# Value products of the first layer: hi and lo weights side by side in two passes, and a bank read per head

## What is computed

```python
p = jax.nn.softmax(logits, axis=-1).astype(v.dtype)
return jnp.einsum('bhqk,bhkd->bhqd', p, v)           # MLA; the MoBA heads likewise
...
mixed = jnp.concatenate([mla_out, moba_out], axis=-1) @ ab_w_out[e]
```

## Time and profile before

| | |
|---|---|
| time, median of 3 runs (lowest to highest) | 1370.87 us (1370.07 to 1371.33) |
| the profiled execution: its own time, its span | 1372.31 us, 1370.5 us |
| busy share: PE, PEld, DVE, ACT, POOL | 95%, 80%, 54%, 40%, 19% |
| mean granted TensorE clock | 0.981 of 2.4 GHz |
| value products of the first layer | 192 matmuls from 95.6 to 278.7 us |

### The profile page before, as it was taken

One profiled execution on the slowest core, in us unless ns is written; L12 is line 12 of the kernel. 1 busy time (PEld: TensorE's weight loads), 2 busy tenths in 40 slices (PEclk: granted clock), 3 DMA queues, 4 the chain that ended last, 5 costly groups with the idle time before them and its releaser, 6 DMA issues.

```text
span 1370.5 us, 17699 instructions
## 1 busy us (share of the span) xinstructions
PE 1308.7 (95%) x6599; PEld 1098.5 (80%) x6599; DVE 744.7 (54%) x997; ACT 553.9 (40%) x885; POOL 258.4 (19%) x206
## 2 busy tenths in 40 slices
PE   7978999999999999999998999987999999999997
PEld 5666888889888888888987888866988888888885
DVE  4776655428654454322386888783475544443223
ACT  4456566546322332222355544453453222322112
POOL 0533100016211111000141112211441111110002
PEclk9989999999999999999999999998999999999998
DMA  5412233122333333333231113110224333333331
GB/s 154 121 29 62 62 85 85 38 86 72 114 92 95 104 92 90 98 94 91 77 88 47 47 46 88 50 47 14 87 73 120 92 94 105 92 107 93 92 93 61
DMA packets 190503, 112.34 MB, mean 82 GB/s; under 512 B 13696, under 2 KB 184773, under 8 KB 190446
## 3 DMA queue, kind: packets, MB, share of 16 engines
q1 hardware_dynamic: 188636, 106.81, 27.1%
q0 software_dynamic: 640, 2.10, 0.5%
q10 hardware_dynamic: 1170, 2.66, 0.5%
HBM read 109.43 MB, written 4.74 MB: 83 GB/s over the span
## 4 chain that ended last, share of the span: by engine, by line
PE 83%; DVE 8%; ACT 4%; issue 2%; POOL 2%; DMA 0%; POOLq 0%; DVEq 0%; ACTq 0%; SPq 0%
PE banks L386 25%; PE banks L388 25%; PE banks L387 25%; PE banks L1661 3%; PE banks L1579 1%; DVE w_lo L381 1%; DVE softplus L1636 1%; PE banks L1408 1%; PE banks L1691 1%; ACT softplus L1620 1%; PE banks L435 1%; DVE u_lo L667 1%; DVE tf L657 1%; DVE logits L1370 0%; POOL rope_tmp L1117 0%
## 5 line engine op out<-in xcount | busy, mean ns | idle before, releaser
L381 DVE TENSOR_TENSOR w_lo<-w_raw,w_hi 128x1024 fp32r<-128x1024 f32 (+2 forms) x200 | 287.1, 1439 | 277.2 <-ACT w_hi L374 277.0
L386 PE MATMUL banks<-u_hi,w_hi 128*128 128x512 f32 (+1 forms) x1112 | 426.0, 383 | 7.4 <-DVE w_lo L381 4.3
L388 PE MATMUL banks<-u_hi,w_lo 128*128 128x512 f32 (+1 forms) x1112 | 419.6, 377 | 0.0
L387 PE MATMUL banks<-u_lo,w_hi 128*128 128x512 f32 (+1 forms) x1112 | 419.2, 377 | 0.0
L374 ACT ACTIVATE w_hi<-w_raw 128x1024 fp32r<-128x1024 f32 (+2 forms) x200 | 205.8, 1030 | 264.2 <-PE banks L388 264.2
L386 PEld LDWEIGHTS banks<-u_hi,w_hi 128*128 128x128 f32 x1112 | 210.5, 189 | 48.3 <-issue 6.8
L388 PEld LDWEIGHTS banks<-u_hi,w_lo 128*128 128x128 f32 x1112 | 210.3, 189 | 38.8
L387 PEld LDWEIGHTS banks<-u_lo,w_hi 128*128 128x128 f32 x1112 | 210.6, 189 | 38.1 <-issue 1.0
L860 POOL TENSOR_TENSOR up<-up,gate 128x512 f32<-128x512 f32 x44 | 71.8, 1632 | 375.5 <-DVE up L886 358.4
L841 ACT ACTIVATE gate<-gate 128x512 f32<-128x512 f32 x44 | 27.8, 632 | 202.3 <-DVE gate L882 202.3
L1678 POOL TENSOR_TENSOR stick_lo<-softplus,stick_hi 128x1280 fp32r<-128x1280 f32 x15 | 44.2, 2948 | 191.4 <-DVE stick_hi L1674 191.4
(11 more groups left out here) (244 smaller groups left out, 2010.0 us busy)
## 6 DMA issues: line engine op xcount, KB each, us to landing
w_raw<-in_ffn_w_gate_up_dram SPq DMA_DIRECT2D x88, 512.0 KB, 3.8
w_raw<-in_ffn_w_down_dram SPq DMA_DIRECT2D x30, 512.0 KB, 3.7
w_raw<-in_sb_w_qkv_dram SPq DMA_DIRECT2D x24, 512.0 KB, 3.9
w_raw<-in_ab_w_in_dram SPq DMA_DIRECT2D x17, 512.0 KB, 3.8
w_raw<-in_ffn_w_down_dram SPq DMA_DIRECT2D x16, 448.0 KB, 3.7
w_raw<-in_ab_w_out_dram SPq DMA_DIRECT2D x8, 512.0 KB, 4.1
w_raw<-in_sb_w_out_dram SPq DMA_DIRECT2D x8, 512.0 KB, 4.9
bias_by_distance<-bias_rows ACTq DMA_DIRECT2D x1, 2560.0 KB
```

The source lines that it names most:

```text
L381: dve.tensor_tensor(wl[:, c.slot, 0:w], raw[:, c.slot, 0:w], wh[:, c.slot, 0:w].bitcast(F32), ALU.subtract).then_inc(w_lo, 1)
L386: nc.tensor.matmul(o, lh, rh, start=start, stop=False, skip_group_check=True)
L387: nc.tensor.matmul(o, lh, rl, start=False, stop=False, skip_group_check=True)
L388: return nc.tensor.matmul(o, ll, rh, start=False, stop=stop, skip_group_check=True)
```

## The change

- The values get one tile `va` with, for each head, 128 columns: v_hi in the head's own 64 columns (64e on) and v_lo in the other 64. The zeros, and GpSimd's two memsets for them, are gone. A filler keeps the other tiles where they were.
- A value product is two passes instead of three, 8 matmuls instead of 12: all 128 columns by probsT_hi, then by probsT_lo. The output bank holds the head's main rows at 64e and the correction rows (v_lo's products) in the other half.
- The bank is started and read for each head by itself. ScalarE copies the main rows to `oh`, and the correction rows to `sqt` at the main rows' place. VectorE subtracts `oh` from the main rows into `acc` (`o_read_dve`, which frees the bank), and then adds `sqt` to give `ol` (`o_dve`). All of these have 64 rows.
- Order: `o_act` stands at the end of every step, not of odd ones; `o_read_dve` for head hh - 1 stands in front of probsT_lo of head hh, and its `o_dve` behind it. Each head's product after the first waits for `o_read` of the head before. `out_pe` waits for `o_dve` of head 15.

```diff
-            vh = sb(at0, "v_hi", [P, 2, TT, 192], F32R)
-            vl = sb(at0, "v_lo", [P, 2, TT, 192], F32R)
+            va = sb(at0, "v", [P, 2, 2, TT, P], F32R)
+            sb(at0, "beside_v", [P, 1024])
...
+        def v_half(buf, e, lo):
+            at = HD * (e ^ lo)
+            return va[:, buf, e, :, at:at + HD]
...
         def pv_pe(pe, hh):
             p, e = hh // 2, hh % 2
             pe.wait_ge(pt_lo, hh + 1)
             if e == 0:
                 pe.wait_ge(pj_read, order[("vt", p, 0)] + 1)
-                if p:
-                    pe.wait_ge(o_lo, p)
-            values(bank(O_BANK), (vh, vl), p % 2, e, pth, ptl, 0).then_inc(pv_done, 1)
+            if hh:
+                pe.wait_ge(o_read, hh)
+            for j in range(TT):
+                w, at = T - P * j, COL_AT[j]
+                for n, x in enumerate((pth, ptl)):
+                    mm = nc.tensor.matmul(bank(O_BANK)[:, P * j:T], va[:, p % 2, e, j, :], x[:, at:at + w],
+                                          start=(j == 0 and n == 0), stop=(j == TT - 1 and n == 1),
+                                          skip_group_check=True)
+            mm.then_inc(pv_done, 1)
+
+        def o_act(act, hh):
+            p, e = hh // 2, hh % 2
+            act.wait_ge(pv_done, hh + 1)
+            act.activation(oh[p][head_rows(e), :], bank(O_BANK)[head_rows(e), :], ACT.Copy)
+            if hh >= 2:
+                act.wait_ge(o_lo, hh - 1)
+            act.activation(sqt[head_rows(e), :], bank(O_BANK)[head_rows(1 - e), :], ACT.Copy).then_inc(o_hi, 1)
+
+        def o_read_dve(dve, hh):
+            p, e = hh // 2, hh % 2
+            dve.wait_ge(o_hi, hh + 1)
+            if hh >= 2:
+                dve.wait_ge(o_lo, hh - 1)
+            nc.vector.tensor_tensor(acc[head_rows(e), :], bank(O_BANK)[head_rows(e), :],
+                                    oh[p][head_rows(e), :].bitcast(F32), ALU.subtract).then_inc(o_read, 1)
+
+        def o_dve(dve, hh):
+            p, e = hh // 2, hh % 2
+            dve.wait_ge(o_read, hh + 1)
+            nc.vector.tensor_tensor(ol[p][head_rows(e), :], acc[head_rows(e), :], sqt[head_rows(e), :], ALU.add)\
+                .then_inc(o_lo, 1)
...
-            pool.wait_ge(consts_ready, 2)
-            for v in (vh, vl):
-                nc.gpsimd.memset(v[:, :, :, HD:2 * HD].bitcast(F32), 0.0)
...
-                if hh % 2:
-                    o_act(act, hh // 2)
+                o_act(act, hh)
...
                 if hh + 1 < NH0:
                     den_dve(dve, hh + 1)
+                if hh:
+                    o_read_dve(dve, hh - 1)
                 probs_dve(dve, hh)
+                if hh:
+                    o_dve(dve, hh - 1)
                 if hh % 2:
                     item_split_dve(dve, a)
                 else:
-                    if hh:
-                        o_dve(dve, hh // 2 - 1)
                     item_split_dve(dve, a)
                     item_scale(dve, a)
...
-            out_pe(pe, CH_OUT0, 0, 0, N_POST_A0, out0_at, (o_lo, MLA_PAIRS + MOBA_PAIRS), (7, 7, 5))
+            out_pe(pe, CH_OUT0, 0, 0, N_POST_A0, out0_at, (o_lo, NH0), (7, 7, 5))
```

More of the change, by code:

```diff
@@ L314, in bass_hybrid_two_layers @@
         pv_done, o_hi, o_lo = sem("pv_done"), sem("o_hi_done"), sem("o_lo_done")
+        o_read = sem("o_bank_read")
         f_read = sem("f_read")
@@ L1195, in n_tf @@
             return tf_of[it[:3]]
-        def v_views(v, buf):
-            return v[:, buf, :, 0:HD], v[:, buf, :, 2 * HD:3 * HD]
+        def v_half(buf, e, lo):
+            at = HD * (e ^ lo)
+            return va[:, buf, e, :, at:at + HD]
         def qk_dst(it):
@@ L1249, in item_act @@
                 src = bank(item_bank(it)).rearrange("p (t h n) -> p t h n", t=TT, h=2)
-                a, b = v_views(vh, p % 2)
-                act.activation(a, src[:, :, 0, :], ACT.Copy)
-                act.activation(b, src[:, :, 1, :], ACT.Copy).then_inc(pj_hi, 1)
+                for e in range(2):
+                    ins = act.activation(v_half(p % 2, e, 0), src[:, :, e, :], ACT.Copy)
+                ins.then_inc(pj_hi, 1)
                 return
@@ L1306, in item_lo @@
                 for x in range(2):
-                    ins = nc.vector.tensor_tensor(v_views(vl, p % 2)[x], src[:, :, x, :],
-                                                  v_views(vh, p % 2)[x].bitcast(F32), ALU.subtract)
+                    ins = nc.vector.tensor_tensor(v_half(p % 2, x, 1), src[:, :, x, :],
+                                                  v_half(p % 2, x, 0).bitcast(F32), ALU.subtract)
                 ins.then_inc(pj_read, 1)
@@ L1421, in probs_dve, with head_rows @@
                 .then_inc(pt_lo, 1)
[L1423 to L1429, removed]
+        def head_rows(e):
+            return slice(HD * e, HD * e + HD)
         def pv_pe(pe, hh):
@@ L1694, in sb_pv_pe @@
             mm.then_inc(sv_done, 1)
-        def head_rows(e):
-            return slice(HD * e, HD * e + HD)
         def so_at(o, p, e):
@@ L2197, in _ @@
                     split_lo(dve, Chunk(CH_OUT0 + AHEAD))
-            o_dve(dve, NH0 // 2 - 1)
+            o_read_dve(dve, NH0 - 1)
+            o_dve(dve, NH0 - 1)
             out_dve(dve, CH_OUT0)
@@ L2286, in _ @@
                     pe.wait_ge(pj_read, len(items))
+                    pe.wait_ge(o_lo, NH0 - 4)
                     out_part(pe, CH_OUT0, 0, out0_at, 0, 6)
@@ L2294, in _ @@
                 item_pe(pe, c)
-            pe.wait_ge(o_lo, NH0 // 2 - 1)
+            pe.wait_ge(o_lo, NH0 - 2)
             for n in range(3):
                 out_part(pe, CH_OUT0, n, out0_at, *((6, 7) if n < 2 else (4, 5)))
-            out_pe(pe, CH_OUT0, 0, 0, N_POST_A0, out0_at, (o_lo, MLA_PAIRS + MOBA_PAIRS), (7, 7, 5))
+            out_pe(pe, CH_OUT0, 0, 0, N_POST_A0, out0_at, (o_lo, NH0), (7, 7, 5))
             gu_pe(pe, CH_GU0, 0, N_FFN0)
```

## The result

The changed kernel took 1376.47 us (median of 8 runs, 1373.38 to 1378.57), the kernel before beside it 1371.1 us (8 runs, 1370.07 to 1373.23): a ratio of 1.0038, 95% interval 1.0027 to 1.005. So it is slower, by 5.4 us. The forecast was 1374.3 us, in a range from 1369.5 to 1377.5 us. The side and the range are right; 2.2 us are missing.

What follows compares the result with a forecast made beforehand. ScalarE and VectorE on the path before 147.5 us, TensorE the bound after. Running sum +5.6, +5.0, +3.1, +2.5, +2.7, with the clock +3.4 us, carried to the 1370.87 median: 1374.3 us, range 1369.5 to 1377.5.

Steps and rivals of the forecast that it cites:

- The MLA steps: Steps 1 to 4: added ScalarE and VectorE work delays step 5's scores product by +5.6 us; TensorE's savings become idle time.
- The rule of the earlier trace for VectorE's halves: VectorE's 64-row operations: pitch 0.61 us in the lower half, 0.72 in the upper, from starting in another partition group.
- rival B: Costs and savings cancel, with pitches of 0.5 and 0.6 us for 64 rows: 1371 us, chance 0.25.
- Rival A: TensorE counts wherever it is busy; ScalarE and VectorE have unseen room: -4.0 us, 1367 us, chance 0.11.
- The wait in step 13: TensorE's first output product waits 1.05 us for v_lo of the last pair, 1.2 with the restart.
- the tail: Behind head 15: copies, o_read and o_dve in series cause a 0.7 us wait; against head 15's saving, +0.2 us.
- MoBA pairs, steps 6 to 11: TensorE waits 0.5 us before k, so each pair gives 0.7 us instead of 1.24: three pairs, -1.9 us.
- Step 5: Delayed scaling of the first MoBA q just uses up k's 2.4 us of room; head 5 still saves 0.6 us.
- Steps 12 to 15: Heads 12 to 14 give 1.87 us, less 1.2 in step 13 and 0.1 for copies: -0.6 us.
- The clock: Step 5's scores product may restart at half clock after idling, costing 1.4 us; one of two, booked as 0.7.
- Rival D: New unpriced waits: whole cold restart, another in MoBA steps or step 13, or late weight split; about 1377 us, chance 0.18.
- C: The forecast itself: 1373.0 us without the cold restart and small terms, 1376.0 with it, chance 0.46.

Runs made afterwards that it cites:

- e1: The kernel before without the third pass (probsT_hi by v_lo) of the first layer's value products, no new reads or copies: 1364.69 us, ratio 0.9952.
- e3: The changed kernel with the two copies of even heads moved behind v_hi of the odd step, still ahead of probsT_hi: 1378.28 us, ratio 1.0044.
- e8: The changed kernel without ScalarE's second copy of each head (the correction rows): 1374.53 us, ratio 1.0025.
- e10: The changed kernel with v_hi copied ahead of the last two exponentials in even steps 6 to 12: 1377.29 us, ratio 1.0042.
- e9: e5 with o_read waiting for the main rows' copy alone, and v_hi ahead of the last two exponentials in even steps 6 to 12: 1367.5 us, ratio 0.9973.
- e7: e3 plus eight matmuls that serve nothing in TensorE's idle time ahead of step 5's scores product: 1372.01 us, ratio 1.0009.
- e2: The changed kernel with a third pass put back (probsT_hi once more), 12 matmuls a head: 1380.26 us, ratio 1.0065.
- e5: The changed kernel reordered: even heads' copies and odd-step o_read behind the weight split, even-step o_read behind probsT_lo, o_dve behind the scalings: 1371.27 us, ratio 0.9995.
- e4: The changed kernel reordered: even heads' copies behind the weight split, odd-step o_read behind the scores and, in MLA steps, q's scaling: 1370.84 us, ratio 0.9999.

## Why the prediction came out as it did

**Right, with their size.** A value product of 8 matmuls takes 1.23 us (forecast 1.25). The MLA steps cost 5.75 us (5.6), and each of them what it was priced at: +1.52, +1.10, +2.01 and +1.12 us for steps 1 to 4 (1.55, 1.0, 2.0, 1.0), between the restarts at 90.99, 114.96, 125.19, 141.14 and 151.38, which stood at 92.89, 115.34, 124.47, 138.41 and 147.53 before. The rule of the earlier trace rows for VectorE's halves held: in step 3 (lower half) the read and the add have pitches of 0.58 and 0.60 us, in step 4 (upper half) 0.73 and 0.72. On ScalarE the two copies have pitches of 0.59 and 0.62, not 0.5. With that rival B falls. Rival A decided at a v_hi less than 0.5 us late in step 3: there are 1.21 us of copies in front of it and no idle time. e1 shows that A, and more, would have come true if the reads had cost nothing. The wait in step 13 is 1.08 (1.05), that for oB_lo at the tail 0.59 (0.7).

**The step that failed** is "MoBA pairs, steps 6 to 11": "the pair gives 0.7 us instead of 1.24". It gave 0.09. From 181.42 to 208.69 and 235.95 the period is 27.27 and 27.26 us. Before, the same matmuls stood at 177.02, 204.39 and 231.75, a period of 27.37 and 27.36, and had no wait:

```profile
177.02 0.50 PE L386 MATMUL banks<-u_hi,w_hi 128*128 128x512 f32 x1
...
231.75 0.50 PE L386 MATMUL banks<-u_hi,w_hi 128*128 128x512 f32 x1
```

That is -0.3 for three pairs where I had -1.9. I followed the copies' delay along probsT_hi, the scores and the scaling to k, and took TensorE to reach k without another wait. In odd steps it meets item b first, the q projection. That goes into bank 7, which holds the transposed v until v_lo has been read, and v_lo is late by the same copies. I had this wait in step 13, where an explicit wait names it, but not in steps 5 to 11. The same omission is in "Step 5": "this 0.6 still comes" (-0.6) was a wait of 0.65 at 154.17. Up to the k projection of step 11 the two make 2.3 us too little. The forecast goes from +5.6 to +3.1 there, the traces from +5.75 to +5.52; these are the matmuls in the kernel before and in the changed one:

```profile
239.19 0.45 PE L386 MATMUL banks<-u_hi,w_hi 128*128 128x512 f32 x1
...
242.81 0.45 PE L387 MATMUL banks<-u_hi,w_hi 128*128 128x512 f32 x1
```

(239.19 - 92.89 = 146.30 us, and 242.81 - 90.99 = 151.82.) Steps 12 to 15 and the tail gave 0.1 less than forecast (-0.32 for -0.4), and the MLA steps cost 0.15 more. That is the stage's 5.20 against 2.7.

e3 takes the v_lo wait away by order alone and has the forecast's period less 0.1 (26.55 for 26.7), so my figure for the path through the scaling was near. e8 takes it down to 0.33 by shortening the copies alone. e10 limits that: once ScalarE waits 0.54 us between the exponentials, with the copies still in front of probsT_hi, the path through the scaling alone takes the whole gain. The copies stand in front of two paths; e9 frees both.

**The clock.** I booked 0.7 us, half of a cold restart. The profiled execution had none at this place; so this part of 1374.3 was no part of its 5.2 us. e3 and e7 show that the risk is real and that I sized it too low: 2.6 us. How often it falls on the changed kernel is open. Of the eight profiled kernels in which this restart came after 2.21 or 2.22 us, five went on at full clock (changed, e2, e5, e9, e10) and three did not (e3, e4, e8), so "one of two" was a fair guess and the size was the error.

**Rival D** (new waits, about 1377 us) names the kind of thing that happened, in the right place, though for it I had priced the clock or weight splits and not v_lo. The measured time lies in D's part of the range, above C's own 1376.0. So the side is right by its mechanism, the MLA steps. The total is as near as it is partly by luck: the 0.7 for the clock stood in for some of the missing wait.

## What to carry to other kernels

When an operation is put in front of a queue, follow its delay to every consumer, and list for each shared buffer who must have read it before the next writer: the first such wait decides, and when it is removed a second one can take a part of its place (0.25 for 1.08 us in e3) or nearly all of it (0.9 in e10). An operation moved out of a busy engine pays only if the ones it adds are placed in the other queues' idle time: the same work in another order, with one wait split (e9), went from 5.4 us slower to 4.0 us faster than before. Late is not safe either: e4 put a read where the next product had to wait for it.

## What the runs showed of the hardware

- Nearly equal waits of TensorE ended differently. In front of step 5's scores product it waited 2.21 or 2.22 us in eight kernels. Over the 4 us behind, the granted clock was 1.00 in the changed kernel, e2, e5, e9 and e10, and 0.50, 0.62 and 0.57 in e3, e4 and e8. Elsewhere it fell after a shorter wait: e5 ran at 0.50 from 124.96 to 126.96 after 1.83 us.
- Eight matmuls without use in an idle time of 2.2 us cost nothing (first part 59.99 against 60.00) and saved 2.6 us of half clock behind it.
- On ScalarE the pitch of a 64-row copy depends on which rows the operation behind it uses. The copy of rows 0 to 63 has 0.48 us in e8, where v_hi, which starts at row 0, follows (178.25 to 178.73, above). It has 0.59 in the changed kernel, where `sqt`'s copy reads from row 64 on, and that one has 0.62 in front of v_hi (124.83 to 125.42 to 126.04). In e8 the upper half's copy has 0.61 (161.24 to 161.85) in front of a copy of 128 rows. The copy of 128 rows out of the same bank in the kernel before has 0.50:

```profile
184.68 0.60 ACT L1445 ACTIVATE oA_hi<-banks 128x512 fp32r<-128x512 f32 x1
185.18 0.62 ACT L1265 ACTIVATE moba_q_hi<-tf 128x512 fp32r<-128x512 f32 x1
```

So it isn't the 64 rows that make the copies dearer. In these rows the 0.1 us comes where neighbours start at different rows, as on VectorE; no run here tries other rows.
